# Early square sums, paired first turns and a two-part condition broadcast in a three-layer kernel on one core

## The chip, the cores and the metric

One core of one Trainium2 chip. The time is device time in microseconds (us) of one execution of the whole program; the median of several executions is compared. Everything is float32 on the outside; the large products run as three products of split halves.

## What is computed

Three transformer layers over 256 tokens of width 1024, one after another on the same `x`. In outline:

```python
for layer in (0, 1, 2):
    sh1, sc1, g1, sh2, sc2, g2 = split(silu(c) @ ada_w + ada_b, 6)
    h = rms_norm(x, norm1) * (1 + sc1) + sh1
    mix = (latent attention over x and ctx, plus a Fourier mix   # layer 0
           gated convolutions over tokens                        # layer 1
           windowed attention over x and ctx_2)(h)               # layer 2
    x = x + g1 * (mix @ w_out)
    h = rms_norm(x, norm2) * (1 + sc2) + sh2
    x = x + g2 * ((silu(h @ w1) * (h @ w3)) @ w2)   # layers 0, 1
    # layer 2: (a * gelu(conv3(g))) @ w_down, with [a, g] = h @ w_up
```

The contexts are normed too, with a shift and scale of their own: `ctx` before layer 0, `ctx_2` for layer 2.

## The kernel before

All activations lie transposed: 128 features to a tile, `KT` = 8 tiles of 256 tokens (`xT`). Weights come as 281 blocks of 128 x 1024 (512 KB), each loaded by SyncE (SP) into a ring of six (`load_w`), then split: ScalarE casts the upper part (`split_hi`, w_hi), VectorE subtracts (`split_lo`, w_lo). A product of float32 is then three TensorE products (`split3`, lines 1621 to 1623). Each engine runs one long list in order; semaphores join the lists. A load into a ring place waits for the split (`split_done`) of the block six back. `split_to(w)` issues all splits up to block w; `LEAD` = 4 is how far the splits run ahead at a stage's end. Some blocks of layer 1 (`WHOLE`) are used unsplit.

**A norm** (eight in all, numbered 0 to 7; 0, 2, 3, 4, 6, 7 are of x, 1 and 5 of the contexts) has these steps:

- ScalarE squares the eight tiles (`square`), as x is updated.
- GpSimd (Pool) adds the first `POOLED[n]` squares into tile 0 (`add_squares`), in the order of `SQ_ORDER`: 0, 1, 5, 2, 3, ...
- TensorE sums over features (`norm_sums`, line 1700), one pair of 1-column products for each remaining tile and one for Pool's.
- ScalarE takes the root (`norm_root`), VectorE the reciprocal (`invert`) and the gain.
- TensorE spreads the result over partitions (`norm_spread`, line 1677).
- For each tile VectorE scales (`scale`, line 1102), ScalarE shifts and casts (h_hi, line 695), VectorE makes the lower part (h_lo, line 1110).

While the root is on its way, `norm(n, rows)` on TensorE fills in something: part of a group of `ada_rows` (the product of the condition with the ada weights; eight blocks k, in four column strips that run side by side, line 1648), or, in norm 7, `hold_clock`, products of nothing (line 1713) that keep the engine busy.

**A feed-forward** runs 11 turns. A turn takes six blocks: `up(0)` and `up(1)` with two each (silu part and gate part, 2 x 8 tiles of x, 48 products each), then two `down` blocks (24 products each) that add into four banks. Between them ScalarE activates, VectorE multiplies (`product`), ScalarE casts g_hi, VectorE makes g_lo (line 1253). In layer 2 the chain is longer: gate copy on ScalarE (line 785), three convolution steps on VectorE (lines 1234, 1238), gelu, product, g_hi, g_lo. At a feed-forward's end VectorE updates x by banks (line 1310). The last turn splits the first four blocks of the next stage.

**The output projection** (`project_out`) starts with four blocks at once (`project_four`), going over the mixed tiles in the order they come; in layer 1 tile 4 is first, and the sum over convolution channels (`conf_sum(1)`) stands behind it.

**The start**: `cond_spread(0)` broadcasts the condition in two halves for VectorE, which makes most ada products by itself (`sum_mod_blocks`, line 1067); four early groups of ada are TensorE's (`ada_rows`, `ada_columns`).

Two lines decide the order in a norm and in a first turn:

```python
ks = ks[1:] + ks[:1] if POOLED[n] < KT - 1 else ks          # L1693, Pool's sum last
if s == 0 and e == 0: pe.wait_ge(hlo_ready, ...)            # L1861, tile by tile, first block only
```

## Time and profile before

| | us |
|---|---|
| median of 3 runs | 1129.73 (1124.77 to 1129.95) |
| the profiled execution | 1125.79 |
| its span in the profile | 1124.0 |
| TensorE busy | 1094.6 (97%) |
| VectorE busy | 777.7 (69%) |
| ScalarE busy | 540.9 (48%) |
| GpSimd busy | 122.6 (11%) |
| mean DMA | 207 GB/s |

### The profile page before, as it was taken

How to read it: one execution, taken by the hardware profiler on the slowest of the kernel's cores; microseconds unless marked ns; L12 is line 12 of the kernel's file. 1: busy time of each engine (PE TensorE's matmuls, PEld its weight loads, DVE VectorE, ACT ScalarE, POOL GpSimd, SP SyncE). 2: the span in 40 equal slices, each digit the busy share in tenths (PEclk: the TensorE clock that was granted, in tenths of full speed). 3: DMA queues.
4: the chain of work that ended last, by engine and by line, in shares of the span. 5: the costliest groups of instructions: out<-in, count | busy, mean ns of one | idle time of the engine just before them, and what ended most of it. 6: DMA issues, size and time to landing. Idle time of an engine off the chain costs nothing.

```text
span 1124.0 us, 21218 instructions
## 1 busy us (share of the span) xinstructions
PE 1094.6 (97%) x8446; PEld 1001.5 (89%) x8446; DVE 777.7 (69%) x1305; ACT 540.9 (48%) x928; POOL 122.6 (11%) x132
## 2 busy tenths in 40 slices
PE   6999999999999999899999999999999999999998
PEld 2889687999999899789999999989775789999998
DVE  2688776788888768656777765747439857666765
ACT  4542566444344575555444445423147746445542
POOL 1201004000000047310000001200331010000000
PEclk9899999999999999999999999999999999999999
DMA  9971373798898625466778775446731044545451
GB/s 364 410 281 58 125 249 114 287 360 326 332 343 335 223 102 199 141 234 225 276 270 291 264 264 168 147 149 208 154 107 45 2 150 150 179 176 204 157 180 38
DMA packets 68596, 232.95 MB, mean 207 GB/s; under 512 B 12144, under 2 KB 12432, under 8 KB 68144
## 3 DMA queue, kind: packets, MB, share of 16 engines
q1 hardware_dynamic: 62496, 227.27, 56.4%
q0 software_dynamic: 5888, 3.73, 1.7%
q10 hardware_dynamic: 144, 1.05, 0.3%
q8 instruction: 43, 0.70, 0.3%
q14 instruction: 25, 0.20, 0.1%
HBM read 230.91 MB, written 1.05 MB: 206 GB/s over the span
## 4 chain that ended last, share of the span: by engine, by line
PE 85%; DVE 8%; issue 2%; DMA 2%; ACT 1%; POOL 1%; SPq 0%; DVEq 0%; POOLq 0%; ACTq 0%
PE bank L1621 24%; PE bank L1623 23%; PE bank L1622 23%; PE bank L2107 2%; DMA a_raw<-ada 2%; PE bank L1774 1%; PE bank L1677 1%; DVE w_lo L1027 1%; DVE bank L1141 1%; PE bank L2156 1%; DVE big L1102 1%; PE bank L1797 1%; PE bank L1700 1%; POOL big L575 1%; PE bank L1669 1%
## 5 line engine op out<-in xcount | busy, mean ns | idle before, releaser
L1621 PE MATMUL bank<-h_hi,w_hi 128*128 128x256 f32 (+1 forms) x1576 | 464.5, 295 | 9.0 <-DVE h_lo L1110 4.7
L1623 PE MATMUL bank<-h_hi,w_lo 128*128 128x256 f32 (+1 forms) x1576 | 456.3, 290 | 0.0
L1622 PE MATMUL bank<-h_lo,w_hi 128*128 128x256 f32 (+1 forms) x1576 | 456.2, 289 | 0.0
L1027 DVE TENSOR_TENSOR w_lo<-w_raw,w_hi 128x1024 fp32r<-128x1024 f32 x271 | 331.6, 1246 | 72.4 <-ACT w_hi L637 71.1
L1621 PEld LDWEIGHTS bank<-h_hi,w_hi 128*128 128x128 f32 x1576 | 304.5, 193 | 24.6 <-issue 13.3
L637 ACT CAST w_hi<-w_raw 128x1024 fp32r<-128x1024 f32 x271 | 277.3, 1046 | 63.6 <-PE bank L1623 54.4
L1622 PEld LDWEIGHTS bank<-h_lo,w_hi 128*128 128x128 f32 x1576 | 304.8, 193 | 3.4 <-issue 0.8
L1623 PEld LDWEIGHTS bank<-h_hi,w_lo 128*128 128x128 f32 x1576 | 304.6, 193 | 2.9
L1621 PE MATMUL bank<-g_hi,w_hi 128*128 128x256 f32 x544 | 153.8, 283 | 0.9 <-DVE g_lo L1253 0.9
L1622 PE MATMUL bank<-g_lo,w_hi 128*128 128x256 f32 x544 | 152.8, 281 | 0.0
L1623 PE MATMUL bank<-g_hi,w_lo 128*128 128x256 f32 x544 | 152.7, 281 | 0.0
L1621 PEld LDWEIGHTS bank<-g_hi,w_hi 128*128 128x128 f32 x544 | 102.5, 188 | 1.4 <-issue 1.1
L1622 PEld LDWEIGHTS bank<-g_lo,w_hi 128*128 128x128 f32 x544 | 102.6, 189 | 0.1
L1623 PEld LDWEIGHTS bank<-g_hi,w_lo 128*128 128x128 f32 x544 | 102.7, 189 | 0.0
L575 POOL TENSOR_TENSOR big<-big 128x256 f32<-128x256 f32 x34 | 39.0, 1147 | 575.1 <-ACT big L683 573.6
L1067 DVE SCALAR_TENSOR_TENSOR a_raw<-a_raw,bias 128x1024 f32<-128x1024 f32 x80 | 97.2, 1219 | 0.2
L780 ACT ACTIVATE work<-bank 128x256 f32<-128x256 f32 x44 | 17.0, 386 | 140.4 <-PE bank L1623 140.4
L1248 DVE TENSOR_TENSOR work<-work,bank 128x256 f32<-128x256 f32 x66 | 27.8, 421 | 76.7 <-ACT work L780 63.3
L695 ACT ACTIVATE h_hi<-big,mods 128x256 fp32r<-128x256 f32 x64 | 30.4, 504 | 42.3 <-DVE big L1102 42.3
L603 POOL TENSOR_TENSOR vals<-vals,work 128x256 f32<-128x256 f32 x48 | 38.8, 808 | 16.4 <-ACT work L932 10.4
L1067 DVE SCALAR_TENSOR_TENSOR a_raw<-a_raw,con 128x1024 f32<-128x1024 f32 x32 | 40.5, 1266 | 0.0
L794 ACT CAST g_hi<-work 128x256 fp32r<-128x256 f32 x66 | 26.8, 406 | 25.5 <-DVE work L1248 24.2
(170 smaller groups left out, 1181.4 us busy)
## 6 DMA issues: line engine op xcount, KB each, us to landing
w_raw<-weights SPq DMA_DIRECT2D x281, 512.0 KB, 4.6
a_raw<-ada SPq DMA_DIRECT2D x140, 512.0 KB, 5.2
vals<-ada SPq DMA_DIRECT2D x4, 512.0 KB, 8.6
a_raw<-rpb POOLq DMA_DIRECT2D x9, 224.0 KB, 18.5
bias<-rpb POOLq DMA_DIRECT2D x7, 224.0 KB, 8.7
xT<-xt SPq DMA_DIRECT2D x1, 1024.0 KB, 10.1
big<-ctx SPq DMA_DIRECT2D x1, 1024.0 KB, 13.5
big<-ctx ACTq DMA_DIRECT2D x1, 1024.0 KB, 6.0
```

What stands on the lines that cost most here:

```text
L575: nc.gpsimd.tensor_tensor(v[:, 0, :], v[:, 0, :], v[:, k, :], ADD).then_inc(added, 1)
L603: nc.gpsimd.tensor_tensor(cacc[:, g, :], first, tap[:, m % TAP_RING, :], ADD).then_inc(pool_taps, 1)
L637: nc.scalar.copy(w_hi[:, s, :], w_raw[:, s, :]).then_inc(hi_done, 1)
L695: nc.scalar.activation(h_hi[:, k, c0:c0 + T], tmp[:, k, :], ACT.Identity, bias=sh).then_inc(hhi_ready, 1)
L794: nc.scalar.copy(g_hi[:, s, :], gate_f[:, s, :]).then_inc(ff_hi, 1)
L1027: nc.vector.tensor_tensor(w_lo[:, s, :], w_raw[:, s, :], w_hi[:, s, :].bitcast(fp), SUB)\
L1067: nc.vector.scalar_tensor_tensor(out=a_raw[:, s, :], in0=a_raw[:, s, :], scalar=1.0, in1=cond_row[later], op0=MUL, op1=MUL, accum_out=flat ...
L1248: nc.vector.tensor_tensor(gate_f[:, s, :], act_f[:, s, :], bank[b][:, half:half + T], MUL)\
L1621: nc.tensor.matmul(out, a_hi, b_hi, start=start, stop=False)
L1622: nc.tensor.matmul(out, a_hi, b_lo, start=False, stop=False)
L1623: return nc.tensor.matmul(out, a_lo, b_hi, start=False, stop=stop)
L2107: ins = nc.tensor.matmul(b[:, 0:T], w_raw[:, w % RING, k * P:(k + 1) * P], h_whole[k], start=(k == 0), stop=(k == KT - 1))
```

## The change

- **First turn by pairs** (`ffn`, TensorE): in turn 0, `up(0)` goes over the normed tiles once and multiplies each by both weight blocks; before, first block over all tiles, then the second.
- **Early squares** (`norm_sums`, `norm`): for norms 2, 4 and 7 the sum of Pool's tile and of all but the last square comes ahead of the filler, the last square behind it. The filler is parted 2, 2, 4 blocks of ada (in norm 2: 2, then 6 behind the spread), hold_clock 3, 2, 6 products (before 3, 2, 4).
- **Context sums behind the second norm's**: `norm_sums(5)` moves from the end of `project_out(0)` to behind the last sum of norm 2, ahead of the spread; Pool adds the squares of norm 2 before those of 5; root and reciprocal follow the same order.
- **The end of feed-forward 0** splits two blocks of the next stage, no longer four. The third is split between squares and root of norm 3 on ScalarE, and between gain and tiles on VectorE; the fourth behind the root and behind the tiles.
- **`project_four`** waits for each block's split by itself.
- **Condition broadcast in two halves**: first half behind `ada_rows(0)`, second among the first products behind tile 3; banks 0 and 2, ScalarE's copies behind the squares of norm 0 and behind its last shift.

```diff
-SQ_ORDER = (0, 1, 5, 2, 3, 4, 6, 7)
+SQ_ORDER = (0, 1, 2, 5, 3, 4, 6, 7)
...
-        place_cond(0, 0)
+        place_cond(0, (0, 2))
...
+            add_squares(2)
             add_squares(5)
-            add_squares(2)
             add_squares(3)
...
                 square(n, KT - 1)
+                norm_root(n)
                 if n == 2:
                     norm_root(5)
-                norm_root(n)
                 norm(n)
...
-                    hi(8, splits_on)
-                    hi(9, splits_on)
+                    hi(8, splits_on and more)
+                    hi(9, splits_on and more)
...
-                hi_next[0] = w0 + 3 * FT + LEAD
+                hi_next[0] = w0 + 3 * FT + (LEAD if layer else 2)
...
-            cond_copy(0)
             ada_copy(0)
             for k in range(KT):
                 square(0, k)
+            cond_copy(0, range(1))
             warm(ACT.Sqrt)
...
             for k in range(4, KT):
                 shift(0, k)
+            cond_copy(0, range(1, 2))
...
             for k in range(KT):
                 square(3, k)
+            split_to(W_IN1 + 2)
             norm_root(3)
+            split_to(W_IN1 + 3)
             norm(3)
...
-                if layer == 0:
-                    invert(("norm", 5))
...
-            norm(2)
+            norm_gain(2)
+            invert(("norm", 5))
+            norm_tiles(2, 0, KT)
             ffn(0)
 
-            norm(3)
+            norm_gain(3)
+            split_to(W_IN1 + 2)
+            norm_tiles(3, 0, KT)
+            split_to(W_IN1 + 3)
...
+            def sum_order(n):
+                return [0, *range(POOLED[n], KT)] if n in (2, 4, 7) else [*range(POOLED[n], KT), 0]
...
             def norm(n, rows=None):
 
+                early, late = ((slice(0, -1), slice(-1, None)) if n in (2, 4, 7) else (slice(0, 0), slice(0, None)))
+                norm_sums(n, early)
                 if rows:
-                    ada_rows(rows, range(3))
+                    ada_rows(rows, range(2))
                 else:
                     hold_clock(6, 3)
-                norm_sums(n)
-                if rows:
-                    ada_rows(rows, range(3, 5))
+                norm_sums(n, late)
+                if n == 2:
+                    norm_sums(5)
+                elif rows:
+                    ada_rows(rows, range(2, 4))
                 else:
                     hold_clock(6, 2)
                 norm_spread(n)
                 if rows:
-                    ada_rows(rows, range(5, KT))
+                    ada_rows(rows, range(2 if n == 2 else 4, KT))
                 else:
-                    hold_clock(6, 4)
+                    hold_clock(6, 6)
...
                 banks = [write_tile(pe, name) for name in names]
-                split_ready(w + len(names) - 1)
                 for k in order:
...
                     for j, b in enumerate(banks):
+                        if k == order[0]:
+                            split_ready(w + j)
...
-                if layer == 0:
-                    norm_sums(5)
-
...
+                        if isinstance(i, int) and i == 0 and s == 0:
+                            pe.wait_ge(split_done, splits_to(ws[1]))
+                            for k in range(KT):
+                                pe.wait_ge(hlo_ready, KT * (2, 4, 7)[layer] + k + 1)
+                                for e in range(2):
+                                    a = wtile(ws[e], k * P, P)
+                                    ins = split3(outs[e], a[0], a[1], xs(h_hi, k), xs(h_lo, k),
+                                                 k == 0 and (e == 0 or layer == 2), k == KT - 1 and (e == 1 or layer == 2))
+                                    if k == KT - 1:
+                                        ins.then_inc(w_used, 1)
+                            return
...
+            ada_rows(0)
             pe.wait_ge(s_con, 16)
-            cond_spread(0)
-            ada_rows(0)
+            cond_spread(0, range(1))
             ada_columns(0)
...
-            first_products(range(3, KT))
+            first_products(range(3, 4))
+            cond_spread(0, range(1, 2))
+            first_products(range(4, KT))
```

## Rows read from the trace of the kernel before

**Rows 1.** The page: TensorE's busy time; its granted clock in 40 slices, in tenths.

```profile
PE 1094.6 (97%) x8446; PEld 1001.5 (89%) x8446; DVE 777.7 (69%) x1305; ACT 540.9 (48%) x928; POOL 122.6 (11%) x132
...
PEclk9899999999999999999999999999999999999999
```

**Rows 2.** Stretches: length, busy PE, PEld, DVE, ACT, POOL, clock, DMA share, GB/s.

```profile
182.70:190.70 8.00, 7.84 (x47) 4.02 (x45) 2.93 (x10) 3.09 (x8) 3.06 (x4) 0.80 0.45 151
...
198.50:382.90 184.40, 184.40 (x1547) 184.31 (x1545) 148.54 (x221) 80.06 (x112) 0.00 (x0) 1.00 0.89 332
```

**Rows 3.** Timeline of TensorE at the start: start, length, line, tiles, [idle <- releaser].

```profile
3.75 3.37 PE L1677 MATMUL bank<-con,cs 128*128 128x128 f32 x16 [3.75 <-ACT cs L825]
...
15.10 2.18 PE L1648 MATMUL bank<-a_raw,cs 128*2 128x512 f32 x8 [1.11 <-DMA a_raw<-ada]
...
36.56 0.38 PE L1621 MATMUL bank<-h_hi,w_hi 128*128 128x256 f32 x1 [1.33 <-DVE h_lo L1110]
```

**Rows 4.** Timeline of TensorE behind norm 4: products of tile 0 and tile 5.

```profile
504.55 0.36 PE L1621 MATMUL bank<-h_hi,w_hi 128*128 128x256 f32 x1 [0.95 <-DVE h_lo L1110]
...
508.40 0.39 PE L1621 MATMUL bank<-h_hi,w_hi 128*128 128x256 f32 x1 [0.16 <-DVE h_lo L1110]
```

**Rows 5.** Timelines of ScalarE and VectorE at norm 2 and its first turn.

```profile
198.08 0.58 ACT L665 COPY ada_s<-bank 128x512 f32<-128x512 f32 x1
198.86 0.39 ACT L780 ACTIVATE work<-bank 128x256 f32<-128x256 f32 x1 [0.20 <-PE bank L1623]
...
188.89 1.26 DVE L1102 SCALAR_TENSOR_TENSOR big<-xT,gain,bank 128x256 f32<-128x256 f32 x3 [1.58 <-PE bank L1677]
...
201.36 0.42 DVE L1253 TENSOR_TENSOR g_lo<-work,g_hi 128x256 fp32r<-128x256 f32 x1
```

**Rows 6.** Timeline of TensorE in norm 2 and at tile 5 behind it.

```profile
182.66 0.95 PE L1700 MATMUL bank<-con,big 128*128 128x1 f32 x8
...
184.50 2.15 PE L1700 MATMUL bank<-con,big 128*128 128x1 f32 x16
...
187.55 1.23 PE L1677 MATMUL bank<-con,stat 128*128 128x128 f32 x4
188.71 1.88 PE L1648 MATMUL bank<-a_raw,cs 128*2 128x512 f32 x6
...
194.54 0.39 PE L1621 MATMUL bank<-h_hi,w_hi 128*128 128x256 f32 x1 [0.17 <-DVE h_lo L1110]
```

**Rows 7.** Timeline of ScalarE (a square); the chain of waits, Pool's adds.

```profile
178.27 0.42 ACT L683 ACTIVATE big<-xT 128x256 f32<-128x256 f32 x1
...
178.44 1.80 POOL big L575
...
184.47 0.73 POOL big L575
```

**Rows 8.** Timelines of VectorE and TensorE at the end of feed-forward 0, norm 3.

```profile
379.65 2.36 DVE L1027 TENSOR_TENSOR w_lo<-w_raw,w_hi 128x1024 fp32r<-128x1024 f32 x2 [0.53 <-ACT w_hi L637]
...
382.00 3.22 DVE L1310 SCALAR_TENSOR_TENSOR xT<-bank,mods,xT 128x256 f32<-128x256 f32 x8
...
384.63 2.36 PE L1700 MATMUL bank<-con,big 128*128 128x1 f32 x20 [0.65 <-ACT big L683]
```

**Rows 9.** Timeline of TensorE, first product of the second output projection.

```profile
463.29 0.36 PE L1621 MATMUL bank<-h_hi,w_hi 128*128 128x256 f32 x1 [1.93 <-DVE w_lo L1027]
```

**Rows 10.** Timelines of TensorE, ScalarE and VectorE at norm 7 and its first turn.

```profile
925.17 3.60 PE L1713 MATMUL bank<-con 128*128 128x512 f32 x8
...
931.10 0.39 PE L1621 MATMUL bank<-h_hi,w_hi 128*128 128x256 f32 x1 [0.16 <-DVE h_lo L1110]
...
944.96 0.36 PE L1621 MATMUL bank<-g_hi,w_hi 128*128 128x256 f32 x1 [0.93 <-DVE g_lo L1253]
...
934.64 0.37 ACT L785 COPY vals<-bank 128x256 f32<-128x256 f32 x1
...
936.38 0.35 DVE L1234 TENSOR_SCALAR work<-vals,taps 128x256 f32<-128x256 f32 x1
```

More of the change, by code:

```diff
@@ L367, in place_rows, with place_cond @@
             place_tile(("columns", g), (3, 4)[n % 2] if n < 4 else 6, (mod_ready, n + 1), (ada_turned, n + 1))
[L369 removed]
+        def place_cond(n, banks):
             for half in range(2):
[L371 removed]
+                place_tile(("cond", n, half), banks[half], (cond_copied, 2 * n + half + 1))
         for g in ROW_GROUPS[:4]:
@@ L665, in ada_copy, with cond_copy @@
                 nc.scalar.copy(ada_s[:], b[:, :]).then_inc(ada_copied, 1)
-            def cond_copy(n):
-                for half in range(2):
+            def cond_copy(n, halves=range(2)):
+                for half in halves:
                     b = wait_tile(act, ("cond", n, half))
@@ L770, in ffn, with turn @@
                 split_to(w0 + LEAD - 1)
-                def turn(i, splits_on=True):
+                def turn(i, splits_on=True, more=True):
                     def hi(j, on=True):
@@ L1221, in ffn, with turn @@
                 split_to(w0 + LEAD - 1)
-                def turn(i, splits_on=True):
+                def turn(i, splits_on=True, more=True):
                     def lo(j, on=True):
@@ L1284, in turn @@
                         shift_low(5, i - 3)
-                    lo(8, splits_on)
-                    lo(9, splits_on)
+                    lo(8, splits_on and more)
+                    lo(9, splits_on and more)
                     if sums > 2 or sums == 1:
@@ L1292, in ffn @@
                     for i in range(FT // 2):
-                        turn(i)
+                        turn(i, more=layer or i < FT // 2 - 1)
                     add_mod_biases(sums_next[0] // AGRP)
@@ L1681, in column, with cond_spread, norm_sums @@
                 return stat[:, c:c + 1].broadcast_to([P, m])
-            def cond_spread(n):
-                for half in range(2):
+            def cond_spread(n, halves=range(2)):
+                for half in halves:
                     spread(("cond", n, half), [cs[:, 2 * n, 4 * half + k, 0:1].broadcast_to([P, P]) for k in range(4)])
-            def norm_sums(n):
-                b = write_tile(pe, ("sum", ("norm", n)))
-                at = SQ_ORDER.index(n)
-                ks = [0, *range(POOLED[n], KT)]
-                ks = ks[1:] + ks[:1] if POOLED[n] < KT - 1 else ks
-                for k in ks:
+            def sum_order(n):
+                return [0, *range(POOLED[n], KT)] if n in (2, 4, 7) else [*range(POOLED[n], KT), 0]
+            def norm_sums(n, part=slice(None)):
+                order = sum_order(n)
+                b = bank[tiles["sum", ("norm", n)][0]]
+                for k in order[part]:
+                    if k == order[0]:
+                        write_tile(pe, ("sum", ("norm", n)))
                     if k:
@@ L1697, in norm_sums @@
                     else:
-                        pe.wait_ge(added, sum(POOLED[m] - 1 for m in SQ_ORDER[:at + 1]))
+                        pe.wait_ge(added, sum(POOLED[m] - 1 for m in SQ_ORDER[:SQ_ORDER.index(n) + 1]))
                     for t in range(2):
                         ins = nc.tensor.matmul(b[:, t:t + 1], sq_of(n)[:, k, t * P:(t + 1) * P], ones,
-                                               start=(k == ks[0] and t == 0), stop=(k == ks[-1] and t == 1))
-                ins.then_inc(full_of(("sum", ("norm", n))), 1)
+                                               start=(k == order[0] and t == 0), stop=(k == order[-1] and t == 1))
+                    if k == order[-1]:
+                        ins.then_inc(full_of(("sum", ("norm", n))), 1)
             def norm_spread(n):
@@ L1853, in up @@
                             write_tile(pe, ("gate", s))
+                        ws = [w0 + 2 * s + e for e in range(2)]
+                        outs = [bank[b][:, e * T:(e + 1) * T] if layer < 2 else bank[b][:, 0:T] if e
+                                else bank[tiles["gate", s][0]][:, 0:T] for e in range(2)]
+                        if isinstance(i, int) and i == 0 and s == 0:
[9 more added lines that the diff above has]
+                            return
                         for e in range(2):
-                            w = w0 + 2 * s + e
-                            pe.wait_ge(split_done, 6 * i + splits_to(w))
-                            out = (bank[b][:, e * T:(e + 1) * T] if layer < 2 else bank[b][:, 0:T] if e
-                                   else bank[tiles["gate", s][0]][:, 0:T])
+                            pe.wait_ge(split_done, 6 * i + splits_to(ws[e]))
                             for k in range(KT):
-                                if s == 0 and e == 0:
-                                    pe.wait_ge(hlo_ready, KT * (2, 4, 7)[layer] + k + 1)
-                                a = wtile(w, k * P, P)
-                                ins = split3(out, a[0], a[1], xs(h_hi, k), xs(h_lo, k),
-                                             k == 0, k == KT - 1)
+                                a = wtile(ws[e], k * P, P)
+                                ins = split3(outs[e], a[0], a[1], xs(h_hi, k), xs(h_lo, k), k == 0, k == KT - 1)
                             ins.then_inc(w_used, 1)
```

11 lines of the change are left out of this document (5 added, 6 removed).

## Prediction

> **What bounds the kernel now.** I read the page's busy line first: TensorE is busy for 1094.6 of 1124.0 us [rows 1]. The second line there, the granted TensorE clock in 40 slices, shows it near full speed nearly everywhere. So only three things can move the time: fewer or faster products, stretches in which TensorE waits, and stretches at half clock. The change removes no product of the model. Then I took stages. A feed-forward layer runs without a gap: 184.40 us busy in 184.40, 1547 products, so 0.119 us each at full clock [rows 2]. The 8 us around norm 2 are different: mean clock 0.80, so 1.6 us worth of clock is lost in it. Last I went through the timelines around each norm, where the idle time stands in brackets with its releaser. All the gain there can be is in the seams: the start, norms 2, 3, 4 and 7, and the entry into the second output projection.
>
> **The start.** The broadcast of the condition was two halves of 8 passes, together 3.37 us, ahead of the first ada rows. It moves: one half behind the first rows, the other among the first products. Its own time can't be won, because the rows behind it wait for their DMA (1.11 us idle before 15.10) and later rows do so too. The half among the products costs half of 3.37, 1.7 us at the pace of 3.75, and falls into the 1.33 us wait for tile 4 (36.56) [rows 3]. If it runs at that pace it sticks out by 0.4 us; a quicker pace makes it free. On ACT the copies move too: the first goes behind the squares of norm 0, the second behind the last shift, where it delays the context squares and Pool's adds of them. Against that stands one gain: less idling before tile 4. I take 0, with bounds of 0.6 us lost and 1.6 us won (a half-clock stretch that goes, priced as in rows 2).
>
> **Turns by pairs.** The first `up` of a feed-forward runs tile 0 of the weights over all eight normed tiles, then tile 1 over them. A normed tile costs VectorE two operations and arrives every 0.77 us (504.55 to 508.40 is five of them), but three products fill only 0.36 us. From tile 5 on (508.40) TensorE is no longer held up, and 33 products remain, to 512.33 [rows 4]. In pairs a tile brings six products, 0.71 us, which fit the 0.77; behind tile 5 only 18 remain. Gain: 15 x 0.119 = 1.79 us. What is late next is g_lo(0), which the down products need. In norm 2: ScalarE splits two blocks, copies ada (198.08 to 198.66), and starts the silu at 198.86, only 0.2 us of that waiting for TensorE; g_lo(0) is ready at 201.36 + 0.42 = 201.78 [rows 5]. So that chain gets only 0.2 us earlier. The second `up` ends 48 products (5.71 us) behind the first: before at 198.47 (194.54 + 33 x 0.119 [rows 6]) + 5.71 = 204.2, now at 202.4 or a little before. The slack is 0.6 to 0.8 us and the gain is kept whole. Norm 4 has the same order; I take 1.8 there, bounds 1.2 and 1.9. Its root comes no earlier: before, three row blocks and four sums stood ahead of it, now three sums, two blocks (as long as three, since blocks run side by side) and one sum.
>
> **Norm 2.** Before: context sums at 182.66, three row blocks, own sums at 184.50 (2.15 us because Pool's adds come last), spread at 187.55, three blocks at half clock 1.88 us [rows 6]. Pool now takes the own adds first. They follow the squares; tile 4's is at 178.27, so with an add beside VectorE's splits (1.80 us [rows 7]) they end near 180.5, in time. Own sums: 12 passes from 182.66 at 0.12 us (2.36 us for 20 [rows 8]), two blocks (0.94), the last sum (0.5): end 185.5, against 186.6 before. But the context sums now stand ahead of the spread and wait for six adds of Pool: two beside VectorE's work at 1.80, four alone at 0.73 and some 0.1 between: 187.3, sums done 187.8. That is later than 187.55, where the spread began. With the clock still at half there, the spread takes 1.23 us, the first scale starts 0.2 us later than at 188.89, six blocks instead of three hold TensorE to 191.8, and 48 products run to 197.5 against 198.5: gain 1.0. At full clock the spread ends at 188.5, blocks and tile 0 meet at 190.4, tile 5 comes at 194.2, the end is 196.4: gain 2.1. I take 1.5. If all six adds ran at 1.80 us beside other work, the spread would start 4.2 us later and this seam would lose some 3 us; VectorE has nothing after 184 but a reciprocal, which speaks against it. The Trainium skill (SBUF — State Buffer, section "SBUF: two separate sides") says VectorE and GpSimd take one port pair as an exclusive lock when VectorE reads two SBUF inputs. By it the waiting grows with VectorE's two-input work, which fits 1.80 against 0.73, and Pool is to pay for every split it meets.
>
> **Norm 3.** VectorE runs two splits from 379.65 to 382.00 ahead of the eight updates of x, which end at 385.22 [rows 8]. They are those of the third and fourth block of the next stage, and move away. The updates then follow the accumulator banks; the last bank is full at 382.9 and its two updates end at 384.1. ScalarE's squares follow by 0.4, so the sums, which waited 0.65 us and took 2.36, end at 386.0 or so instead of 387.0: gain 1.0. The two splits land where their engines wait: one between square and root on ScalarE (TensorE is still summing) and between gain and scale on VectorE (TensorE spreads), one behind the norm's tiles. SP's loads of the blocks in those ring places wait for the later splits, by up to 13 us for the second, and whatever is behind them in the queue; these blocks are used five projections on or later. Bounds 0.5 (a split of 1.2 us half visible) and 1.2.
>
> **Entry of the second output projection.** The first product waits 1.93 us for the fourth weight block's split, since all four were waited for together [rows 9]. Now each is waited for by itself. Nine products (1.07 us) of three blocks go into the wait; the three left end 1.07 us earlier at full clock. In the trace the 12 products and what follows ran partly at half clock, so 1.8 is what I take. Behind it TensorE is busy up to the squares' sums of the second half, and a chain over ScalarE hangs on these. Bounds 1.1, and 2.9 if the half clock goes too.
>
> **Norm 7.** Here the pair buys nothing. Six filler products of two passes, 0.43 to 0.45 us a pass, instead of four follow the spread: 8 passes took 3.60 us from 925.17, 12 end near 930.3. Then 48 products run to 936.1; before it was 931.10 + 33 x 0.119 = 935.0 [rows 10]. The gate copy on ScalarE moves from 934.64 to about 936.1, and with it the convolution, which VectorE could start at 936.38 only: it moves by 0.1. From there gelu, product and split set g_lo(1), for which TensorE already waits 0.93 us before 944.96. So -0.1, bounds -1.0 and +0.2.
>
> **Sum.** 0 + 1.5 + 1.0 + 1.8 + 1.8 - 0.1 = 6.0 us. The lows give 2.2, the highs 10. The profiled execution took 1125.79 us, so 1119.8 against its own time. The three timed runs have their median at 1129.73 and their lowest at 1124.77: the profiled one lies 3.9 below the median, a scatter of the size of the gain. From the median it would be 1123.7. I take the middle, 1121.8.
>
> **Rivals.** (1) The chain behind the pairs. In norms 2 and 4 TensorE reaches the down products early and waits for g_lo(0), as it does now in norm 7. It decides once ScalarE or VectorE is 0.8 us later than I read. Price: up to 3.6 of the 6.0; 1123.4 on the profiled time, 1125.3 on my middle. For: silu waits only 0.2 us for TensorE. Against: the slack computed above. (2) The clock, slower than before. The seams hold small products and waits, and they now lie in another order; the context sums wait for Pool, norm 7 waits longer. A half-clock stretch costs 1.6 us [rows 2]. It decides when four more appear than before; with six, 9.6 - 6.0 = 3.6 us are lost, 1129.4 on the profiled time, some 1131 on my middle. Against: norms 4 and 7 hold such work now and run at full clock. The Trainium skill (TensorE: Matmul & The Clock Gate, Part 1) says that activity releases the throttle and that idling brings it back; the row with 0.80 agrees. (3) The clock comes back: the half-clock stretches after the start's wait, in norm 2 and after the 1.93 us wait go, because the waits go. Three times 1.6, less what is counted above, gives some 3.5 us more: 1116.3 and 1118.3. (4) It doesn't do what it says: the early squares buy nothing. In norms 4 and 7 that is already in the sum, at norm 2 it is 0.5.
>
> **Chances.** Forecast 0.60, rival 1 0.20, rival 2 0.07, rival 3 0.13. The likeliest's own range is 1118 to 1125, the scatter of the base included; with the others 1116.0 to 1127.5. A measurement of this kernel can tell about 0.5% (5.6 us) from no change, and 6.0 lies just beyond it. Forecast above the bound a little over half, rival 3 nearly always, rival 1 seldom: faster 0.54, within 0.40, slower 0.06.
>
> **What would show it.** Right: no bracketed waits between a norm's tiles; first silu after norm 4 without TensorE as releaser; sums before the first in1 products starting near 383.9; the wait at the second output projection cut to about 0.9; norm 7's wait for g_lo at 0 to 1 us before both down halves. Wrong: TensorE waiting for g_lo in the first turn of layers 0 and 1, a context sum that waits over 2 us for Pool, or more than seven half-clock stretches.

## The result, and the profile after

| | before | after |
|---|---|---|
| median of 12 runs each, us | 1126.75 (1123.01 to 1130.83) | 1119.86 (1117.76 to 1122.62) |
| ratio, 95% interval | | 0.9938 [0.9926, 0.9951] |
| profiled execution, us | 1125.79 | 1118.5 |
| its span, us | 1124.0 | 1116.7 |

The kernel is 0.62% faster, 7.0 us, a little above the 0.5% that can be told from no change. The page of the changed kernel, TensorE's busy line and the granted clock in 40 slices, to set beside [rows 1]:

```profile
PE 1091.6 (98%) x8450; PEld 996.0 (89%) x8450; DVE 777.9 (70%) x1305; ACT 540.6 (48%) x928; POOL 118.6 (11%) x132
...
PEclk9999999999999999999999999999999999999999
```

The span fell by 7.3 us and TensorE's busy time by 3.0. So 4.3 us are idle time that went. Busy time holds two things that go against each other: the same products at a better clock, and four more filler passes. Where that happened is read seam by seam (a seam is the stretch between two stages, in which TensorE has little large work): the time from the end of the last product ahead of a seam to one fixed instruction behind it, in both traces. Norm 2 first, TensorE (start, length, line, tiles, [idle <- releaser]), which answers [rows 6]:

```profile
181.21 1.40 PE L1709 MATMUL bank<-con,big 128*128 128x1 f32 x12
182.53 1.03 PE L1654 MATMUL bank<-a_raw,cs 128*2 128x512 f32 x4
183.49 1.05 PE L1709 MATMUL bank<-con,big 128*128 128x1 f32 x8
185.39 0.60 PE L1709 MATMUL bank<-con,big 128*128 128x1 f32 x4 [0.84 <-POOL big L575]
185.86 1.08 PE L1683 MATMUL bank<-con,stat 128*128 128x128 f32 x4
186.87 3.13 PE L1654 MATMUL bank<-a_raw,cs 128*2 128x512 f32 x12
189.93 0.38 PE L1627 MATMUL bank<-h_hi,w_hi 128*128 128x256 f32 x1
...
207.22 0.95 PE L1665 MATMUL bank<-con,ada_s 128*128 128x2 f32 x8
```

From 189.93 on, no product waits for a normed tile; [rows 6] shows such a wait, of 0.17 us, at tile 5, and the kernel before has the like at tiles 2, 3 and 4. The fixed instruction is the last row (ada_columns(24), behind the first turn): 26.01 us after the seam began, before 27.44. Norm 4, same columns, answering [rows 4]:

```profile
489.65 1.40 PE L1709 MATMUL bank<-con,big 128*128 128x1 f32 x12
...
491.93 0.61 PE L1709 MATMUL bank<-con,big 128*128 128x1 f32 x4
...
496.05 0.36 PE L1627 MATMUL bank<-h_hi,w_hi 128*128 128x256 f32 x1 [0.94 <-DVE h_lo L1113]
...
513.59 0.95 PE L1665 MATMUL bank<-con,ada_s 128*128 128x2 f32 x8
```

23.94 us, before 25.83. The entry of the second output projection (squares of the first convolution half, first product, conf_sum(1), and the row blocks behind the first four blocks), answering [rows 9]; the same rows of the kernel before, but for the one that stands there, come second:

```profile
452.50 0.95 PE L1675 MATMUL bank<-con,work 128*128 128x1 f32 x8
...
457.93 0.36 PE L1627 MATMUL bank<-h_hi,w_hi 128*128 128x256 f32 x1 [0.92 <-DVE big L1558]
...
459.44 1.06 PE L2106 MATMUL bank<-vals,con 128*128 128x512 f32 x2
...
473.29 1.04 PE L1654 MATMUL bank<-a_raw,cs 128*2 128x512 f32 x8
```

```profile
456.85 0.95 PE L1669 MATMUL bank<-con,work 128*128 128x1 f32 x8
...
465.43 1.91 PE L2085 MATMUL bank<-vals,con 128*128 128x512 f32 x2
...
481.69 1.04 PE L1648 MATMUL bank<-a_raw,cs 128*2 128x512 f32 x8
```

20.79 us, before 24.84: 4.05 less, the largest piece. But conf_sum(1) took 1.91 us before and 1.06 after, the same two products. The stretches view (length, busy PE, PEld, DVE, ACT, POOL, clock, DMA share, GB/s) of the kernel before shows why:

```profile
463.90:467.40 3.50, 3.50 (x13) 2.46 (x13) 2.70 (x5) 2.00 (x3) 0.00 (x0) 0.51 0.82 323
477.50:481.00 3.50, 3.50 (x20) 3.50 (x19) 1.27 (x3) 1.69 (x4) 0.00 (x0) 0.52 0.23 95
```

Both run at the lower of TensorE's two levels, 1.2 GHz; the changed kernel has 1.00 all through here in this execution. The remaining seams and stretches close the balance of the two profiled executions:

| piece | before | after | difference |
|---|---|---|---|
| up to the sums of norm 1 | 43.95 | 42.34 | -1.6 |
| norm 2 to ada_columns(24) | 27.44 | 26.01 | -1.4 |
| norm 3 (row blocks at 382.95 / 380.07) to ada_columns(25) | 14.72 | 14.74 | 0.0 |
| stretch 399 to 403 us, half clock before only | | | -1.5 |
| entry of the second output projection | 24.84 | 20.79 | -4.0 |
| norm 4 to ada_columns(27) | 25.83 | 23.94 | -1.9 |
| stretches 691 to 695 and 838 to 841, half clock after only | | | +3.2 |
| norm 7 (918.65 / 911.38) to turn 1 | 29.23 | 29.23 | 0.0 |

The half-clock stretches, found by going through the granted clock in steps of half a microsecond: seven before (at 37, 47.5, 187.5, 399, 464, 477.5 and at the very end), five after (22, 186, 384, 691, 838; a sixth begins only behind the last instruction). Each costs 1.5 to 1.6 us where TensorE is busy, as the rows of the table show where nothing but the clock differs (399 to 403, 691 and 838). So much of the 7.3 us can't be laid to an edit by these two executions alone; the experiments had to part that.

### The profile page after: what moved, and what is told of

Its sections match the earlier page's. It is cut to its first block, busy times and chain, and to the rows that moved or that the text cites. A ratio compares the mean times of both kernels' runs of the same rounds, so it can differ in the third digit from the quotient of the medians.

```text
span 1116.7 us, 21196 instructions
## 1 busy us (share of the span) xinstructions
PE 1091.6 (98%) x8450; PEld 996.0 (89%) x8450; DVE 777.9 (70%) x1305; ACT 540.6 (48%) x928; POOL 118.6 (11%) x132
## 3 DMA queue, kind: packets, MB, share of 16 engines
q10 hardware_dynamic: 144, 1.05, 0.3%
HBM read 230.91 MB, written 1.05 MB: 208 GB/s over the span
## 4 chain that ended last, share of the span: by engine, by line
PE 87%; DVE 6%; DMA 3%; issue 2%; ACT 1%; POOL 1%; SPq 0%; DVEq 0%; POOLq 0%; ACTq 0%
PE bank L1627 24%; PE bank L1628 24%; PE bank L1629 24%; PE bank L2128 2%; DMA w_raw<-weights 2%; PE bank L1654 2%; DMA a_raw<-ada 2%; PE bank L1789 2%; PE bank L1683 1%; DVE bank L1144 1%; PE bank L2177 1%; PE bank L1812 1%; PE bank L1675 1%; DVE w_lo L1030 1%; PE bank L1723 1%
```

## Experiments

Each kernel is compared with the kernel before on the same chip in the same session. Between sessions the kernel before moved from 1124.71 to 1127.88 us, so kernels of different sessions are compared by their ratios and not by their medians. The two kernels with tiny activations ran once each (1117.37 and 1120.74 us) and are read by their traces alone.

| kernel | median, us (runs) | ratio to before [95%] |
|---|---|---|
| pairs alone | 1122.21 (12) | 0.9976 [0.9964, 0.9988] |
| block waits alone | 1123.84 (12) | 0.9975 [0.9962, 0.9988] |
| moved splits alone | 1124.63 (12) | 0.9993 [0.9979, 1.0007] |
| order of the sums alone | 1124.02 (11) | 0.9988 [0.9976, 1.0000] |
| condition alone | 1124.38 (12) | 1.0000 [0.9987, 1.0013] |
| four fillers in norm 7 | 1119.61 (4) | 0.9957 [0.9942, 0.9971] |
| filler in Pool's wait | 1119.12 (7) | 0.9944 [0.9924, 0.9964] |
| spread first | 1117.61 (5) | 0.9936 [0.9923, 0.9949] |
| late sum at once | 1115.01 (4) | 0.9889 [0.9872, 0.9905] |
| both of these | 1113.25 (4) | 0.9868 [0.9851, 0.9885] |

### One part at a time

**Pairs alone.** Lines of the change around the first `up`:

```diff
+                        if isinstance(i, int) and i == 0 and s == 0:
+                            pe.wait_ge(split_done, splits_to(ws[1]))
+                            for k in range(KT):
+                                pe.wait_ge(hlo_ready, KT * (2, 4, 7)[layer] + k + 1)
+                                for e in range(2):
...
```

> The kernel before with one part of the change: in the first turn of each feed-forward layer the first up runs over both weight tiles at each normed tile (pairs). Forecast: 15 products' time at norm 2 and at norm 4, 1.8 us each, and nothing at norm 7, so -3.6 us (1126.8 to about 1123.2), with no TensorE wait for g_lo in the first turns of layers 0 and 1; columns(24) and columns(27) start 1.8 us earlier after their norm than in the kernel before. Rival 1 (chain behind the pairs): TensorE waits for g_lo(0) there, up to 1.8 us each, and the total moves by 0 to -1. Rival on the clock (the placement of half-clock stretches is not tied to any part): the seam gains as forecast, while the total of one execution also moves by multiples of 1.6 us in places that this part does not touch.

Measured -2.7 us (-4.1 to -1.4). Norm 4, the spread and ada_columns(27):

```profile
498.13 0.71 PE L1677 MATMUL bank<-con,stat 128*128 128x128 f32 x4
...
518.29 0.95 PE L1659 MATMUL bank<-con,ada_s 128*128 128x2 f32 x8
```

That is 20.16 us, where before it took 22.03 (501.93 to 523.96): 1.87 gained. TensorE waits for no g_lo in the first turns of layers 0 and 1. At norm 2 the seam took 26.95 us against 27.44, with two half-clock stretches in it (185 to 192.5) where the kernel before has one. At norm 4 the pairs are worth what was forecast; at norm 2 the two seams aren't at like clock and don't tell. Rival 1 is out for these two layers.

**Block waits alone.**

```diff
-                split_ready(w + len(names) - 1)
...
+                        if k == order[0]:
+                            split_ready(w + j)
```

> The kernel before with one part: in the projection of four blocks at a time each block's split is waited for by itself. Forecast: 9 products (1.07 us) go into the wait ahead of the second output projection, which shrinks from 1.93 to about 0.9 us, and up to 1.8 us in all: -1.1 to -1.8. Clock theory: of the 4.05 us that this stretch gave in the trace of the changed kernel, about 1.0 is the wait and 3 are two half-clock stretches, which come and go by themselves; then this part alone gives -1.0 in the mean of many executions. Cause theory (the shorter wait keeps the clock up): the two stretches at 464 and 478 us are gone here too, and the total falls by 3 to 4.

Measured -2.8 us (-4.3 to -1.4). TensorE at the entry, in this kernel, and then in the kernel with the moved splits alone, whose entry is that of the kernel before but ran at full clock:

```profile
457.32 0.95 PE L1669 MATMUL bank<-con,work 128*128 128x1 f32 x8
...
462.75 0.36 PE L1621 MATMUL bank<-h_hi,w_hi 128*128 128x256 f32 x1 [0.92 <-DVE big L1552]
...
478.11 1.04 PE L1648 MATMUL bank<-a_raw,cs 128*2 128x512 f32 x8
```

```profile
456.39 0.95 PE L1674 MATMUL bank<-con,work 128*128 128x1 f32 x8
...
462.84 0.36 PE L1626 MATMUL bank<-h_hi,w_hi 128*128 128x256 f32 x1 [1.94 <-DVE w_lo L1029]
...
478.15 1.04 PE L1653 MATMUL bank<-a_raw,cs 128*2 128x512 f32 x8
```

At like clock the seam is 20.79 us with the single waits and 21.76 with the common one: 0.97 us. The other 3.1 of the 4.05 is clock, and it also went in two kernels in which the entry is unchanged (moved splits alone, order of the sums alone). So the shorter wait isn't needed for it. The measured mean is 1.8 us more than the 1.0, which lies just outside its interval; why is open. The fourteen traces of all kernels give a hint and no more. With the common wait, a half-clock stretch began within 1.2 us of the first product in three of five; with single waits in none of nine. But 12 us on, behind TensorE's 1.69 us wait for h_lo, it began in five of those nine and in one of those five.

**Moved splits alone.**

```diff
+            split_to(W_IN1 + 2)
             norm_root(3)
+            split_to(W_IN1 + 3)
             norm(3)
...
-            norm(3)
+            norm_gain(3)
+            split_to(W_IN1 + 2)
+            norm_tiles(3, 0, KT)
+            split_to(W_IN1 + 3)
```

> The kernel before with one part: the splits of the third and fourth block of the second input projection are moved from the end of feed-forward 0 into and behind norm 3. Forecast: the squares' sums of norm 3 start 0.7 to 1.0 us earlier and the total falls by 1.0 (0.5 to 1.2). Rival (as in the trace of the changed kernel, where this seam gave 0.0): the split between gain and scale of norm 3 or the first product takes it back; then the total does not move and the first in1 product comes no earlier after the end of the layer, at the same clock.

Measured -0.8 us (-2.4 to +0.8): the time alone doesn't tell. The seam does, at like clock. Norm 3 to ada_columns(25), with a half-clock stretch in both: 14.84 us here (383.87 to 398.71), 15.64 in the kernel with the order of the sums alone (383.06 to 398.70), which has norm 3 as before. At full clock it took 14.72 before, and 14.14 in the kernel with the filler in Pool's wait, which has the moved splits:

```profile
379.55 1.03 PE L1654 MATMUL bank<-a_raw,cs 128*2 128x512 f32 x4
...
393.69 1.02 PE L1665 MATMUL bank<-con,ada_s 128*128 128x2 f32 x8 [0.91 <-ACT ada_s L665]
```

So 0.6 to 0.8 us. The 0.0 of the changed kernel was a half-clock stretch (384 to 387.5) laid over that.

**Order of the sums alone.**

```diff
-                norm_sums(n)
-                if rows:
-                    ada_rows(rows, range(3, 5))
+                norm_sums(n, late)
+                if n == 2:
+                    norm_sums(5)
+                elif rows:
+                    ada_rows(rows, range(2, 4))
```

> The kernel before with one part: early sums of squares in norms 2, 4 and 7, two and two row blocks or six filler products, Pool's own adds first, the context sums behind norm 2's own. Forecast: norm 2 by itself gains 0 to 0.3 us here, since without the pairs tile 0's products still go at the pace of the normed tiles; norm 4 gains 0 to 0.2 (spread starts 0.1 to 0.2 us earlier); norm 7 loses 0 to 0.2. Sum 0, bounds -0.8 and +0.5. What the traces of before and after say in addition: the spread of norm 2 comes 1.45 + 0.2 us earlier in the changed kernel (185.86 against 187.55, all but 0.24 us of it by the earlier start), so this part should leave the spread within 0.3 us of where it was after the last out product.

Measured -1.4 us (-2.7 to 0). Spread of norm 2: 5.06 us after the last product (182.69 to 187.75), against 4.89 before: within the 0.3 of the forecast. The seam took 27.51 us with two half-clock stretches in it, 27.44 before with one. What the order gives at norm 4 is seen by taking the pairs away from the change: 1.89 for all of it, 1.87 for the pairs alone. The interval of the mean reaches from nothing to 2.7 us; no seam of the trace shows a gain.

**Condition alone.**

```diff
+            ada_rows(0)
             pe.wait_ge(s_con, 16)
-            cond_spread(0)
-            ada_rows(0)
+            cond_spread(0, range(1))
...
-            first_products(range(3, KT))
+            first_products(range(3, 4))
+            cond_spread(0, range(1, 2))
+            first_products(range(4, KT))
```

> The kernel before with one part: the two halves of the condition's broadcast moved, one behind the first ada rows, one among the first products. Forecast: 0 (0.6 lost to 1.6 won). Theory from the two traces: the half among the products took 1.05 us instead of the 1.7 priced, so it fits the 1.33 us wait for tile 4 and costs nothing, and the sums of norm 1 start 1.6 us earlier only because no half-clock stretch falls on the first products; then the mean of many executions moves by 0 to -0.5. Rival (the moved half fills the wait and so keeps the clock up): no half-clock stretch between 35 and 45 us, and the total falls by 1.4 to 1.6.

Measured 0.0 (-1.5 to +1.5). The half among the products took 1.05 us at 34.35 and tile 4 came at 36.42 here, 36.42 in the changed kernel, 36.56 before. So the order itself costs and gives nothing. This trace has no half-clock stretch between 35 and 45 us, as the rival says, and norm 1's sums at 42.35; but it has one at 45 to 48.5, and the time doesn't fall. The 1.6 us that the changed kernel shows ahead of norm 1 are no gain in the mean.

The five ratios add up to -0.68%, the whole gives -0.62%. Within what these intervals leave open (0.12 to 0.14 points for each part), nothing shows that the parts hinder or help each other.

### The slack behind the pairs

```diff
                         ada_copy((24, 27)[layer])
+                        for _ in range(5):
+                            warm(ACT.Silu)
```

In the second kernel it is `range(12)`.

> The changed kernel with five tiny activations (about 1.1 us on ScalarE) ahead of the first silu of layers 0 and 1. By the slack read from the trace of the changed kernel (second up ends at 189.93 + 96 x 0.119 = 201.35 against g_lo(0) at 199.56: 1.8 us at norm 2; 507.5 against 506.82: 0.66 us at norm 4), TensorE does not wait for g_lo at norm 2 and waits about 0.45 us at norm 4. If g_lo were already the bound (rival 1), both would wait 1.1 us; if the slack were wide, neither would.

> The changed kernel with twelve tiny activations, about 2.6 us on ScalarE, ahead of the first silu of layers 0 and 1. With five of them (1.17 us) TensorE had no wait for g_lo at norm 2 and lost 0.25 us at norm 4. By the same slack (1.8 and 0.7 to 0.9 us) TensorE now waits some 0.8 to 1.1 us for g_lo at norm 2 and 1.8 to 2.2 us at norm 4. If g_lo were no path at all, neither would wait.

The five took 1.17 us. TensorE had no wait for g_lo at norm 2; at norm 4 the way from spread to ada_columns(27) took 20.42 us instead of 20.17, so 0.25 of 1.17 came through. With twelve, TensorE of that kernel, norm 2 and norm 4:

```profile
202.59 0.36 PE L1629 MATMUL bank<-g_hi,w_hi 128*128 128x256 f32 x1 [0.78 <-DVE w_lo L1032]
...
513.21 0.36 PE L1629 MATMUL bank<-g_hi,w_hi 128*128 128x256 f32 x1 [1.68 <-DVE w_lo L1032]
```

These are the first down products. The releaser named is the split that VectorE runs just ahead of g_lo(0); the product needs both. At the pace of the five, 0.234 us each, the twelve take 2.8 us; so the slack is 2.0 us at norm 2 (1.8 read) and 1.1 at norm 4, or 0.9 by the kernel with five (0.7 read). The changed kernel is inside it, so rival 1 fails by its slack, not by its mechanism.

### Norm 7's fillers

```diff
-                    hold_clock(6, 6)
+                    hold_clock(6, 4)
```

> The changed kernel with four filler products of two passes behind norm 7's spread instead of six. Forecast theory (norm 7's end hangs on the chain gate copy, convolution, gelu, split, with TensorE just busy to the end): first products near 922.1 instead of 923, gate copy 0 to 0.9 us earlier, end of the first turn within 0.3 us: 0. Rival (the filler is on the path): the total falls by 0.9. Second rival (the filler keeps the clock up): a half-clock stretch appears behind norm 7, +1.6.

Against the changed kernel the seam doesn't move: turn 1 begins 29.23 us after norm 7's first sum in both. What the filler took is what TensorE waits otherwise. Its timeline in this kernel:

```profile
911.48 1.40 PE L1709 MATMUL bank<-con,big 128*128 128x1 f32 x12
...
933.79 0.36 PE L1627 MATMUL bank<-g_hi,w_hi 128*128 128x256 f32 x1 [0.69 <-DVE w_lo L1030]
...
937.80 0.36 PE L1627 MATMUL bank<-g_hi,w_hi 128*128 128x256 f32 x1 [0.93 <-DVE g_lo L1254]
...
940.71 0.28 PE L1627 MATMUL bank<-h_hi,w_hi 128*128 128x256 f32 x1
```

0.69 + 0.93 us of waiting in place of four passes of 0.43. No half-clock stretch came with it. The ratios, 0.9957 and the changed kernel's 0.9938, have intervals that overlap. At norm 7 the end is set by a chain through ScalarE and VectorE, as forecast.

### Where that chain begins

```diff
+                at_once = n in (4, 7)
                 norm_sums(n, early)
+                if at_once:
+                    norm_sums(n, late)
                 if rows:
                     ada_rows(rows, range(2))
                 else:
-                    hold_clock(6, 3)
-                norm_sums(n, late)
+                    hold_clock(6, 1 if at_once else 3)
...
-                    hold_clock(6, 6)
+                    hold_clock(6, 2 if at_once else 6)
```

> The changed kernel with the late sum of norms 4 and 7 right behind the early ones: in its trace square 7 is done at 912.58 and the early sums at 912.63, but the late sum starts at 915.29, behind six filler passes (norm 4: square done at 490.85, early sums at 491.0, late sum at 491.93, behind two row blocks). Fillers of norm 7 become 2 passes ahead of the spread and 4 behind it instead of 10 and 12. Theory (the place of the late sum sets root, spread and scales, and at norm 7 also the chain of gate copy, convolution, gelu and split): norm 7's spread comes 3.0 to 3.4 us earlier behind the last out product, first product from 922.65 to about 916.4, gate copy held by ScalarE's splits and 4.5 us earlier, TensorE waits again for g_lo, about 1.3 and 1.0 us: gain 4.0 to 4.6 there; norm 4: the 0.94 us wait for h_lo goes, gain 0.8 to 0.9. Sum -5.4 against the changed kernel (to about 1114.5). Rival (early sums buy nothing, the chain is bound elsewhere, as forecast for norms 4 and 7): the total moves by less than 1. Rival of the clock: with less filler a half-clock stretch falls on norm 7, 1.6 us of the gain lost.

In the changed kernel the last square of norm 7 and its root on ScalarE lie far apart, and TensorE's late sum is what the root waits for:

```profile
912.16 0.42 ACT L683 ACTIVATE big<-xT 128x256 f32<-128x256 f32 x1 [0.95 <-DVE xT L1216]
915.89 0.26 ACT L657 ACTIVATE stat<-bank,eps 128x2 f32<-128x2 f32 x1 [3.32 <-PE bank L1709]
```

TensorE with the late sum at once:

```profile
910.95 1.85 PE L1709 MATMUL bank<-con,big 128*128 128x1 f32 x16
912.67 1.11 PE L1723 MATMUL bank<-con 128*128 128x512 f32 x2
913.61 0.61 PE L1683 MATMUL bank<-con,stat 128*128 128x128 f32 x4
...
916.13 0.36 PE L1627 MATMUL bank<-h_hi,w_hi 128*128 128x256 f32 x1 [0.19 <-DVE h_lo L1113]
...
929.84 0.36 PE L1627 MATMUL bank<-g_hi,w_hi 128*128 128x256 f32 x1 [1.68 <-DVE w_lo L1030]
...
933.84 0.36 PE L1627 MATMUL bank<-g_hi,w_hi 128*128 128x256 f32 x1 [0.93 <-DVE g_lo L1254]
...
936.75 0.28 PE L1627 MATMUL bank<-h_hi,w_hi 128*128 128x256 f32 x1
```

Spread 2.66 us after the first sum instead of 6.07 (3.41 earlier); turn 1 after 25.80 us instead of 29.23 (3.43 earlier). The whole advance of the spread is kept. The edit does two things here. The late sum starts 1.38 us behind the first instead of 3.91, which is 2.53 of the 3.41; the other 0.88 us is between late sum and spread, where two filler passes stand instead of four. No run parts the two. I had expected 4.0 to 4.6, because the gate copy waits 1.18 us for TensorE in the changed kernel; but VectorE's two splits ahead of the convolution hold it, and they move with the scales only. Norm 4: 22.91 us instead of 23.94, the 0.94 us wait is gone. Together 4.5. The ratios differ by 0.49 points, 5.5 us, with intervals that leave room for 2.4 to 9.

### Norm 2, and what the clock does there

The changed kernel, with norm 2's spread behind two row blocks and ahead of the context sums:

```diff
-                if n == 2:
-                    norm_sums(5)
-                elif rows:
+                if rows:
                     ada_rows(rows, range(2, 4))
                 else:
                     hold_clock(6, 2)
                 norm_spread(n)
+                if n == 2:
+                    norm_sums(5)
...
+            norm_tiles(2, 0, KT)
             invert(("norm", 5))
-            norm_tiles(2, 0, KT)
```

Pool's adds of the context roll into the last tile added, so that scale(2, 0) may overwrite the first.

> The changed kernel with norm 2 in another order: own sums, two row blocks, late own sum, two row blocks, spread, context sums, four row blocks; the context's adds roll into the last of the added tiles, so that the scale of tile 0 can overwrite the first; its root and reciprocal come behind. Expected if the context sums' wait for Pool (0.84 us) and their 8 passes stand on the norm's chain: the spread starts near 184.8 instead of 185.86 (same start of the sums), the first product 1.0 to 1.2 us earlier, and the total falls by 1.0 to 1.2 against the changed kernel (1119.9 to 1118.8). Rival (TensorE's own row blocks are the bound): the spread comes earlier, but the first product doesn't, and nothing is gained. Norm 2 held one or two half-clock stretches in each kernel so far, so the step in the trace is to be read at like clock.

The seam took 23.93 us (181.31 to 205.24) against 26.01, at full clock throughout, with the first product 6.38 us after the last one ahead (187.69) instead of 8.72. The 2.1 us of this trace don't show in the mean: its ratio is 0.9936 [0.9923, 0.9949], that of the changed kernel 0.9938. The second kernel puts one filler into the wait for Pool:

```diff
                 if n == 2:
+                    write_tile(pe, ("inv", 2))
+                    hold_clock(5, 1)
                     norm_sums(5)
```

> The changed kernel with one dense filler product (two passes, about 0.9 us) between norm 2's late sum and the context sums, where TensorE waits 0.84 us for Pool's last add. In the traces so far norm 2's seam held a half-clock stretch wherever that wait stood, save one of another order, and none in the two kernels with the context sums behind the spread. Theory A (TensorE's idling there brings the lower clock): the seam runs at full clock, the row blocks behind the spread take 3 x 1.03 instead of 3.1 to 3.6 us, and the total falls by about 1.6. Theory B (the small products of the seam bring it, or nothing in the seam does, and the two kernels were free of it by chance): a half-clock stretch falls on the seam still and the total stays within 0.3 of the changed kernel.

Its trace is what theory A expects, the clock of norm 2 first in the changed kernel, then in this one:

```profile
186.00:189.50 3.50, 3.50 (x16) 1.02 (x16) 2.69 (x8) 2.00 (x5) 0.00 (x0) 0.51 0.00 0
```

```profile
186.00:189.50 3.50, 3.47 (x25) 1.71 (x25) 2.28 (x7) 1.64 (x5) 0.10 (x1) 1.00 0.01 4
```

The seam took 24.73 us (181.96 to 206.69). But no gain shows in the time: its ratio is 0.9944 [0.9924, 0.9964] where the changed kernel has 0.9938 [0.9926, 0.9951]. A gain of 1.6 us, 0.0014, would lie within these intervals, so the time decides nothing between A and B. And with the late sum at once in norms 4 and 7, where norm 2 is that of the changed kernel, the spread ran at full clock (0.69 us at 187.11) and the lower clock came only at 188. Of the fourteen traces, the three without a half-clock stretch in norm 2 are those in which TensorE doesn't stop for Pool between norm 2's sums; but in the kernel before, and in four of its variants, it doesn't stop there either, and all five had one. What brings the lower clock into a given seam is not settled. What the traces bear out: norm 2 at full clock with the wait filled is 24.73, with the context sums behind the spread 23.93, so that order is worth 0.8 us by itself in the traces, the size of Pool's 0.84 us wait.

**Both together,** the late sum at once in norms 2, 4 and 7, in norm 2 the spread behind two row blocks, then two more row blocks and the context sums:

```diff
+                at_once = n in (2, 4, 7)
...
+                norm_spread(n)
+                if rows and at_once:
+                    ada_rows(rows, range(2, 4))
                 if n == 2:
                     norm_sums(5)
```

> The late sum right behind the early ones in norms 2, 4 and 7, and norm 2's context sums behind its spread, with two row blocks between. By the traces so far norm 2's first product starts at 187.7 with TensorE busy throughout (as with the spread first), so the earlier late sum adds nothing on TensorE there. Expected: the gains of both kernels add, 2.0 and 5.4, -7.4 against the changed kernel (to about 1112.5); if the clock decides, the sum differs by multiples of 1.6.

```profile
181.82 2.11 PE L1716 MATMUL bank<-con,big 128*128 128x1 f32 x16
183.86 1.03 PE L1660 MATMUL bank<-a_raw,cs 128*2 128x512 f32 x4
184.81 0.71 PE L1689 MATMUL bank<-con,stat 128*128 128x128 f32 x4
185.45 1.03 PE L1660 MATMUL bank<-a_raw,cs 128*2 128x512 f32 x4
186.41 1.05 PE L1716 MATMUL bank<-con,big 128*128 128x1 f32 x8
187.39 1.04 PE L1660 MATMUL bank<-a_raw,cs 128*2 128x512 f32 x8
188.36 0.39 PE L1633 MATMUL bank<-h_hi,w_hi 128*128 128x256 f32 x1
```

No wait is left in norm 2. The kernel took 1113.25 us where the one before took 1127.88 in the same session, 1.32% less, and its interval lies clear of the changed kernel's, though not of that of the late sum at once. It is the fastest of these kernels: 8 us below the change by the two ratios (0.9868 and 0.9938 of 1127.88).

## Why the prediction was right, and where it wasn't

The total, -6.0 forecast and -7.0 measured (-8.3 to -5.5), has the right size; its composition less so. Read at like clock, the seams give some 5.0 us: norm 2 1.4, norm 3 0.6 to 0.8, the entry 1.0, norm 4 1.9. The other 2 us of the mean stand in no seam and stay open, so that 6.0 came out so near is in part luck. The forecast time, 1121.8, was 1.9 us above the measured median, half of it because the base was taken at 1127.8 and had its median at 1126.75.

- **Pairs** [rows 4 to 6]. Right: 1.8 forecast, 1.87 measured alone at norm 4, and neither layer waits for g_lo. The slack at norm 2 was 1.8 to 2.0 us and not 0.8, since the whole norm came earlier and ScalarE with it.
- **Norm 2** [rows 6, 7]. 1.4 measured for the 1.5 taken, but the step inside was off: Pool's last add released TensorE 4.18 us after the last product where I had 4.64, since its adds beside VectorE's splits took 1.40 to 1.72 us and not 1.80; the four with VectorE idle took 0.73, as said. So the spread came 0.24 us earlier and not later. The seam stayed at half clock behind it, for which I had priced 1.0.
- **Norm 3** [rows 8]. The sums started 0.96 us behind the row blocks, as forecast (383.9 - 382.95), and the 0.65 us wait for the squares went. Worth 0.6 to 0.8 where I took 1.0. The row blocks at 382.95 took 1.03 us and the sums 2.36 [rows 8], so the sums could end at 386.3 at best and not at 386.0: 0.7 us. TensorE's wait for h_lo ahead of the first product grew from 0.95 to 1.17 us at full clock and takes part of that back. In the profiled execution a half-clock stretch hid it.
- **Entry of the second output projection** [rows 9]. The wait fell to 0.92 us, as said, and at like clock it gives 0.97 us, near the 1.07 of the nine products. I had taken 1.8, a share for half clock included; the same entry ran at full clock in two kernels, with the old common wait, so that share isn't the edit's by any trace. The mean of this part alone, 2.8 (1.4 to 4.3), holds the 1.8 and not the 1.0. So whether the share was wrong is not shown.
- **Norm 4.** 1.9 for 1.8. That the early sums buy nothing there, as rival 4 says, is shown by 1.89 against 1.87.
- **Norm 7** [rows 10]. 0.0 in the trace for -0.1, and by the mechanism given: TensorE's filler and its waits trade one for one.
- **Start** [rows 3]. 0, as forecast; the half broadcast took 1.05 us and not 1.7, since the pace of 3.75 was that of the half clock (see the last section).
- **Rival 3, the clock comes back,** is what the two profiled executions seem to show at the entry (3.1 us), and two stretches further on take as much again (3.2). In the mean only the block waits hint at it, whose -2.8 is more than the 1.0 of its seam. Rival 2 did not come: five stretches, not more than seven.

The Trainium skill (TensorE: Matmul & The Clock Gate, Part 1) ties the clock to activity. Norm 2 with its wait filled ran at full clock in the trace, which agrees. The entry of the kernel before, instruction for instruction, ran at half clock in three traces (before, pairs alone, condition alone) and at full clock in two (moved splits alone, order of the sums alone); activity alone doesn't tell these apart. The Trainium skill's other rule (SBUF — State Buffer, section "SBUF: two separate sides") would have Pool pay for each split beside it: adds of 1.40 to 1.72 us beside splits against 0.72 to 0.73 with VectorE idle agree.

## What to carry to other kernels

Ask of each filler that covers a wait whether it stands ahead of the instruction that ends the wait: here fillers held back a sum whose input was ready 2.7 us before, and moving it, with fewer fillers behind it, gave more than any part of the change. Compare a seam with the same seam at the same granted clock, from any kernel that has it; a difference of two single executions mixes an edit with half-clock stretches of 1.6 us each. And price a shortened wait as the wait, and name apart what is added for the clock next to it: here no trace ties the two, while the mean leaves it open.

## What the hardware showed beyond that

- TensorE's first work runs at the pace of the lower level, though the view prints 1.00. The trace's clock record of the kernel before begins only at 6.57 us. The 16 broadcast passes of [rows 3] start 0.21 us apart up to 6.45 and 0.11 us apart from 6.62 on, which is how 3.37 us came about, while eight of them took 1.05 later (34.92 in the changed kernel). In the changed kernel, whose record begins at 11.92, the first row blocks take what they take at 0.51 elsewhere (1.87 us at 186.15 with the pairs alone), and 1.03 later:

```profile
5.96 1.87 PE L1654 MATMUL bank<-a_raw,cs 128*2 128x512 f32 x4 [5.96 <-DMA a_raw<-ada]
```

  So the pace of a group at the start is no price for it later. And TensorE reaches the full pace later where its first work starts later: at 6.6 to 8.8 us in the five traces with the old start, whose first product comes at 3.6 to 3.8, and at 9.1 to 12.1 in the nine with the moved broadcast, whose first comes at 5.8 to 6.9.
- The lower clock falls on the same seams again and again, but not each time. Of fourteen traces eleven had it in norm 2 (five of them for twice as long, as from 185 to 192.5 with the pairs alone) and ten in norm 3; none had fewer than three such stretches in all.
